# Second half of the value projection moved into the attention's steps, attention output in its own memory, one output bank

## What is computed

```python
q, k, v = jnp.split(h @ w_qkv, 3, axis=-1)          # h: normed tokens; q and k normed by head
# x tokens: neighbourhood plus context
s_nb = einsum('bhqd,bhqkd->bhqk', q_r, k_nb) * NA_SCALE + bias_r
s_ctx = einsum('bhqd,bhkd->bhqk', q_r, kc) * NA_SCALE
p = softmax(concatenate([s_nb, s_ctx], axis=-1))
o = einsum(p[..., :nb], v_nb) + einsum(p[..., nb:], vc)
yx = merge_heads(o) @ w_o
# context tokens (not in layer 3): softmax(qc kc) vc, @ w_o
```

## Time and profile before

| | us |
|---|---|
| median of 3 runs (lowest, highest) | 2507.7 (2506.68, 2511.91) |
| profiled execution, first to last instruction | 2503.2 |
| TensorE busy in it | 2433.3 (97%) |
| DVE / ACT / POOL busy | 1816.1 / 1065.2 / 652.6 |
| heads of layer 0 (203.6 to 302.9) | 99.3 |
| heads of layer 3 (2218.5 to 2279.8) | 61.3 |

### The profile page before, as it was taken

The page is one execution under the profiler, slowest core; times in us unless marked ns, Lnnn a source line. Parts: engine busy times, 40 slices in busy tenths (PEclk is TensorE's granted clock), DMA queues, the critical chain, the costliest instruction groups (busy, mean ns, idle before and its releaser), DMA issues. The chain is left out here.

```text
span 2503.2 us, 36222 instructions
## 1 busy us (share of the span) xinstructions
PE 2433.3 (97%) x12655; PEld 2003.5 (80%) x12655; DVE 1816.1 (73%) x2653; ACT 1065.2 (43%) x1679; POOL 652.6 (26%) x442
## 2 busy tenths in 40 slices
PE   7998899999999999999999999999999999998999
PEld 4675588888888868888888888778888888867999
DVE  4886569888974355427888768987988876855874
ACT  3335534443231244414444227863544324455543
POOL 2414233332300020022333224844333324101000
PEclk9999999999999999999999999999999999999999
DMA  7642025555633321224545542213555554312555
GB/s 270 178 167 76 10 84 171 173 172 192 220 103 101 103 74 51 96 98 135 174 169 173 181 142 77 67 33 111 169 175 168 185 176 125 120 51 68 186 183 186
DMA packets 94890, 337.48 MB, mean 135 GB/s; under 512 B 11840, under 2 KB 13632, under 8 KB 94656
## 3 DMA queue, kind: packets, MB, share of 16 engines
q1 hardware_dynamic: 67136, 240.38, 28.7%
q10 hardware_dynamic: 24768, 86.74, 10.5%
q0 software_dynamic: 2880, 8.92, 1.7%
HBM read 334.95 MB, written 1.05 MB: 134 GB/s over the span
## 5 line engine op out<-in xcount | busy, mean ns | idle before, releaser
L672 PE MATMUL bank<-Hhi,Whi 128*128 128x512 f32 (+1 forms) x2416 | 866.2, 359 | 25.2 <-DVE Wlo L1568 8.4
L674 PE MATMUL bank<-Hhi,Wlo 128*128 128x512 f32 (+1 forms) x2416 | 853.5, 353 | 0.0
L673 PE MATMUL bank<-Hlo,Whi 128*128 128x512 f32 (+1 forms) x2416 | 853.1, 353 | 0.0
L1568 DVE TENSOR_TENSOR Wlo<-raw,Whi 128x1024 fp32r<-128x1024 f32 x424 | 636.4, 1502 | 225.0 <-ACT Whi L1186 207.2
L1186 ACT ACTIVATE Whi<-raw 128x1024 fp32r<-128x1024 f32 x424 | 448.1, 1059 | 749.2 <-DMA raw<-in_weights 695.4
L672 PEld LDWEIGHTS bank<-Hhi,Whi 128*128 128x128 f32 x2416 | 457.1, 189 | 104.1 <-issue 30.5
L673 PEld LDWEIGHTS bank<-Hlo,Whi 128*128 128x128 f32 x2416 | 457.4, 189 | 63.8 <-issue 2.6
L674 PEld LDWEIGHTS bank<-Hhi,Wlo 128*128 128x128 f32 x2416 | 457.4, 189 | 63.0
L545 POOL TENSOR_TENSOR cond_w<-cond_w,cond 128x1024 f32<-128x1024 f32 x107 | 259.3, 2423 | 599.8 <-DVE square L1592 514.7
L672 PE MATMUL bank<-Ghi,Whi 128*128 128x512 f32 (+1 forms) x770 | 268.5, 349 | 0.0
L674 PE MATMUL bank<-Ghi,Wlo 128*128 128x512 f32 (+1 forms) x770 | 266.7, 346 | 0.0
(11 more groups left out here) (267 smaller groups left out, 2990.8 us busy)
## 6 DMA issues: line engine op xcount, KB each, us to landing
raw<-in_weights SPq DMA_DIRECT2D x424, 512.0 KB, 3.4
cond_w<-in_ada ACTq DMA_DIRECT2D x160, 512.0 KB, 3.8
ada_raw<-in_ada SPq DMA_DIRECT2D x16, 512.0 KB, 16.0
ada_ring<-in_ada SPq DMA_DIRECT2D x16, 512.0 KB, 7.4
rel_in<-in_rpb POOLq DMA_DIRECT2D x48, 128.0 KB, 4.8
decay_t<-in_dist POOLq DMA_DIRECT2D x4, 640.0 KB, 4.3
X<-in_x ACTq DMA_DIRECT2D x1, 2048.0 KB, 10.7
out_y<-X SPq DMA_DIRECT2D x1, 1024.0 KB, 4.8
```

What stands on the lines that cost most here:

```text
L672: t.matmul(dst, Whi[:, st.slot, w], hi, start=start, stop=False)
L673: t.matmul(dst, Whi[:, st.slot, w], lo, start=False, stop=False)
L674: return t.matmul(dst, Wlo[:, st.slot, w], hi, start=False, stop=stop)
L1568: v.tensor_tensor(Wlo[:, st.slot, :], raw[:, st.slot, :], Whi[:, st.slot, :].bitcast(F32), ALU.subtract)\
```

## The change

It does four things.

1. Only the first half of V (channels 0 to 511, groups `v+0` to `v+3`) is made ahead of the heads (`values_early`). The second half is made inside the heads' steps, one token block after the other, in bank 7: `late_values(n)`, item n of 32, is one chunk of one block, three matmuls. Layer 0 takes 3, 3, 2 and then 2 items a step, steps 0 to 14; layer 3 takes 3, 3, 2 four times, steps 0 to 11. One item stands between scores and turns, the others behind the turns. ACT alone takes each finished block out (`evict_late`), at the start of its step 3, 7, 11 and 15 (layer 0) or 3, 6, 9 and 12; the next block's first item waits for it.
2. The weight groups `v+4` to `v+7` are all needed until the last block, so their slots come free only then. The splits of `o+0` to `o+2` move to ACT's steps 17, 19, 21 (layer 0; before: two, in steps 5 and 9) and 13, 14, 15 (layer 3; before: none in the heads). DVE follows one step later.
3. The idle transposes are gone. Attend results go to a new tensor `Out` in the place of Q and K, always through bank 6, so an attend waits for the result of the attend **directly** before it.
4. Four of the eight hosted slices move from the value projection and the heads to the output projection's tiles 0, 1, 3 and 4 (`IN_V`, `IN_O`), unshared.

```diff
-IN_V = 8
-V_LATE = 2
-LATE_SPLITS = (5, 9)
+IN_V = 4
+OUT_SPLITS = ((17, 19, 21), (13, 14, 15))
-IN_O = ()
+IN_O = (0, 1, 3, 4)
...
+        self.fill = (3, 3, 2) * TB if self.last else (3, 3, 2) + (2,) * 12
...
+            def values_early(first, tile0):
...
-                tokens_major(p["v"], 2, p["mix_tile"] + 16)
+                values_early(p["v"], p["mix_tile"] + 16)
...
+                def late_values(n):
+                    b, k = divmod(n, C)
+                    st = Step(p["v"] + 4 + k // 2)
+                    if b == 0:
+                        pe.wait_ge(lo_split, st.n + 1)
+                    elif k == 0:
+                        pe.wait_ge(v_made, v0 + 2 + b)
+                    tk = slice(P * b, P * b + P)
+                    last = three_moving(bank[7][:, :], st, slice(512 * (k % 2), 512 * (k % 2) + 512),
+                                        Hhi[:, k, tk], Hlo[:, k, tk], k == 0, k == C - 1)
+                    if b == TB - 1 and k % 2:
+                        last.then_inc(weights_used, 1)
+                    elif k == C - 1:
+                        last.then_inc(v_block, 1)
...
-                    if h.group(n) >= 2:
-                        pe.wait_ge(h_ready, p["o_ready"] + h.group(n) - 1)
+                    if h.group(n) >= 1:
+                        pe.wait_ge(h_ready, p["o_ready"] + h.group(n))
+                    if i >= C // 2:
+                        pe.wait_ge(v_made, v0 + 2 + TB)
...
                     if s == 0:
                         pe.wait_ge(tile_free, FREE0 + p["mix_tile"] + 2 * C + TB)
-                    if s == 1:
-                        pe.wait_ge(tile_free, FREE0 + p["mix_tile"] + 2 * C + 2 * TB)
                     for n in (2 * s, 2 * s + 1):
                         if n < h.n:
                             scores(n)
-                    if s < 4:
-                        idle_products(16 if s == 3 else 5)
+                    items = h.items(s)
+                    for n in items[:1]:
+                        late_values(n)
                     for n in (2 * s - 6, 2 * s - 5):
                         if 0 <= n < h.n:
                             turn(n)
+                    for n in items[1:]:
+                        late_values(n)
...
+                def evict_early():
+                    act.wait_ge(weights_used, p["v"] + 4)
...
+                def evict_late(b):
+                    if b == TB - 1:
+                        act.wait_ge(weights_used, p["v"] + 8)
+                    else:
+                        act.wait_ge(v_block, (TB - 1) * j + b + 1)
+                    a.activation(V[:, b, 512:1024], bank[7][:, :], ACT.Copy).then_inc(v_made, 1)
...
+                evict_early()
+                split(Step(p["v"] + 4))
                 if layer == 0:
-                    evict_v(1)
+                    sum_products(3)
+                    reload(3, p["cond_end"])
...
                 for s in range(h.n // 2 + 5):
+                    if h.block_after(s) is not None:
+                        evict_late(h.block_after(s))
...
+                    if s in h.splits:
+                        split(Step(p["v"] + 5 + h.splits.index(s)))
...
+            def values_early(first, hosts, made):
+                for quarter in range(4):
+                    split(Step(first + quarter))
+                    if hosts:
+                        weigh(quarter, hb[:, :, :].rearrange("p k t -> p (k t)"), follows=quarter >= COND_SLOTS)
+                dve.wait_ge(weights_used, first + 4)
+                for b in range(2):
+                    v.tensor_copy(V[:, b, 0:512], bank[V_BANKS[0][b]][:, :]).then_inc(tile_free, 1)
+                dve.wait_ge(v_made, made + 2)
+                dve.sem_inc(tile_free, 2)
+                split(Step(first + 4))
...
-                    v.tensor_tensor(Hlo[:, i, hs], bank[h.out_bank(i, stream)][:, 0:CTX], Hhi[:, i, hs].bitcast(F32),
+                    v.tensor_tensor(Olo[:, i, hs], bank[6][:, 0:CTX], Ohi[:, i, hs].bitcast(F32),
                                     ALU.subtract).then_inc(h_ready, 1)
```

83 lines of the change are left out of this document (36 added, 47 removed).

## The result

| | before | after |
|---|---|---|
| median of 6 runs, us | 2507.59 (2505.44 to 2511.91) | 2514.72 (2512.36 to 2515.74) |
| profiled execution | 2503.2 | 2510.3 |
| TensorE busy | 2433.3 | 2429.3 |
| DVE / ACT / POOL busy | 1816.1 / 1065.2 / 652.6 | 1820.8 / 1062.0 / 648.6 |

The changed kernel takes 1.003 of the time before, 95% interval 1.0021 to 1.004: slower by 7.1 us, where the prediction said +1.3 and gave the larger chance to "no difference". The time lies in the stated range, 2499 to 2518, but above the forecast's own part of it (2503 to 2512.7): it fell where rival 2, with 2516.5, was expected. Nine more runs of the changed kernel in a later comparison gave 1.0026 (1.0016 to 1.0036).

What follows compares the result with a forecast made beforehand. TensorE, busy 97%, was taken as the bound. Layer 0's +2.3 and layer 3's -0.7 gave +1.6 on the median 2507.7: 2509 us, chance 0.51, own range 2503 to 2512.7, whole range 2499 to 2518.

Steps and rivals of the forecast that it cites:

- rival 2: Single bank becomes the loop of unfilled steps, attends each waiting 0.75 us: +7.5, 2516.5 us; chance 0.23 shared with rival 3.
- Gross gain and start: Filling slack gains 21.5 us gross; heads start 16.8 us earlier in layer 0, 20.2 in layer 3.
- Clock: Layer 0's gap of 5.1 us brings half the clock for 3.4 us, losing 1.7 us; bounds 0 and 3.4.
- Filled steps: Steps 0 to 14 of layer 0 take 54.8 us, steps 0 to 11 of layer 3 53.4, small waits included.
- joints between kinds of matmul: In filled steps, changing from one kind of matmul to another costs 0.7 us in each layer, for some 15 changes.
- Splits: Weight splits in unfilled steps cost 4.2 us in layer 0, 2.5 in layer 3; sum 6.7, bounds 1 and 10.1.
- One output bank: Attends wait for the result directly before, 0.4 us each for five in layer 0, plus both ends: 3.7 us, bounds 1 and 9.
- Hosted slices in the output projection: Four slices make DVE run over by about 1.2 us per tile, unnoticed by TensorE: taken as 0, bound 1.3.
- The rule weighed there: DVE and GpSimd share a port pair under exclusive lock; all eight slice passes would wait for POOL once, sum 1.3 us higher.
- Rival 1: Loop absorbs the splits (6.7 becomes 1) and block boundaries cost nothing (2.8 becomes 0.5): 2501 us; chance 0.26.
- Rival 3: Starts aren't hidden and the fill fails, nothing gained in filled steps: +15 us and more; chance 0.23 shared with rival 2.
- the signs named for a right prediction: TensorE idle 5 and 1.8 us, clock near 0.5, filled steps near 55 and 53, split pairs 12.5 or more, attends waiting for `out_low`.

Runs made afterwards that it cites:

- Evictions ahead of the hosted slice: Changed kernel, in layer 0 evictions of V's first half put ahead of slice 2's sum (ACT) and slice 3's weighing (DVE): 2512.82 us, ratio 1.003.
- holding the clock: Changed kernel plus 36 unread transposes between layer 0's first half of the value projection and the first scores: 2512.37 us, ratio 1.0022.
- the run with fewer joints: The kernel called together, with each step's late items in one run ahead of its turns: 2503.07 us, ratio 0.9984 of the kernel before.
- together: Changed kernel with two output banks after the late items, splits in steps 31, 33, 35 and 15, 17, 19, evictions ahead of split `v+6`: 2497.55 us, ratio 0.9966.

## Why the prediction was right or wrong

**Gross gain and start.** Right. The heads start 16.8 and 20.2 us earlier, with gaps of 5.0 and 1.6 us for 5.1 and 1.8 predicted. The reason given for layer 0's gap was only part of it, as `Evictions ahead of the hosted slice` shows: a split whose load is late stands there too.

**Clock.** The mechanism is right, the size isn't: 1.7 us taken from the earlier trace rows, 2.7 us measured by holding the clock. The lower level lasted 6.8 us, not 3.4, and 6.0 of them lay behind the gap. The bound, 3.4, held. Five other profiles of the same code paid 1.5 to 2.9. And the earlier trace rows shows what came in some profiles only: the wait of 2.25 us of the earlier trace rows is there in all thirteen profiles, and the lower level follows it in five.

**Filled steps.** Layer 0 took 57.7 for 54.8 us. Without the clock's part, 55.0 for 53.1: of 4.4 us beyond the needed 50.6, the three waits for evictions are 2.5 (predicted 1.8) and 1.9 are spread over the steps, 0.1 in a step like that from 239.83 to 243.37 (3.54 us for 3.41 of work; I took 0.7 in all). I named that last part joints between kinds of matmul, and the run with fewer joints doesn't bear it out; its cause stays open. Layer 3: 54.2 for 53.4.

**Splits.** 4.2 and 2.5 us predicted, 3.3 and 1.1 measured. The mechanism is right, and the middle of the heads is the wrong place. By place, the pair with steps 18 to 21, in which the splits of steps 17 and 19 fall, costs 1.1 where I took 2.5, and the next, with step 21's, 2.1 where I took 1.7. Part of it was only covered by the single bank: with two banks layer 0's splits cost 4.5. Layer 3's run into the heads' end, where most of them is hidden.

**One output bank.** 3.7 us predicted, 4.1 measured in the changed kernel (2.9 and 1.2) and 5.4 in the kernel before. Wide attends wait too, which I had at 0, and the last attend of each layer waits 0.9 to 1.0 us longer than before for 0.7. Splits and bank together were taken at 10.4, and are 7.4 + 2.3 = 9.7 with what they cover for each other (the rest of both layers in together against the changed kernel). That this sum came out is partly luck: the edits taken singly give 4.4 for the splits, 2.3 less than I took, and 4.1 for the bank, 0.4 more, and the 1.2 us that each covers for the other were in no term.

**Hosted slices in the output projection.** Taken as 0, measured 1.2, the bound was 1.3. The splits there are indeed far enough ahead, but I looked at TensorE's tiles and not at the norm behind them, which waits for POOL's last sum. The rule weighed there gave +1.3, near what was measured, though four of the eight passes waited for POOL, the second of each slice, and not all eight.

**Rivals.** Rival 1 fell: the splits aren't absorbed. Rival 2 gave 2516.5, close to what was measured, and yet isn't the cause. Its wide and narrow attends all wait, as it said, for 8.2 us in 14 waits, but the price is 4.1, or 5.3 with the splits at the end (layer 0's rest 60.8 to 56.7, layer 3's 25.9 to 24.7), and not 11.2, since part of those waits stands in the place of others. The point from which it decides, 0.3 us more per attend than counted, wasn't reached (4.1 against 3.7 counted is 0.03 for each of 13, 5.3 is 0.12). Rival 3 fell too: the filled steps took 2.9 and 0.8 us more than predicted, not 15. A slip in rival 1: the waits at block boundaries that it lets go were counted with 3.5 us in all (0.4, 1.4, 1.0 and 0.7), not 2.8. The slower result is a sum of small under-estimates on one side: 1.0 (clock), 1.9 (filled steps of layer 0), 0.8 (of layer 3), 1.2 (output projection), and 0.6 outside the stretches; the gaps and the rests of the two layers come out even.

Of the signs named for a right prediction all came but one, filled steps near 55 us in layer 0. Two mechanisms were missed or misplaced, the wait of the norm for POOL and the waits of the wide attends, and the 1.9 us spread over layer 0's filled steps have no known cause. Clock, small waits and slices were taken in the lower part of their bounds, and nothing in the trace said that their errors would cancel.

## What to carry to other kernels

When work is woven into the slack of a loop, price what it pushes out: here the fill itself worked, and the order of the small pieces around it (evictions behind a late load and hosted work, splits in the middle of the heads, one bank for all results) cost more than it gained; with those three put right the same change gains 0.3 to 0.4%. Look for whoever waits behind a stage, not only in it: DVE's lateness in the output projection showed up in the norm. And a wait seen in a trace is not its price, until a run without it shows what comes up behind it.

## What was not expected of the hardware

- The same idle gap of 5.0 to 5.3 us brought 3.4 us at the lower clock in one profile and 6.8 us in five, in these five starting 0.5 to 2.9 us before the gap's end; the price ran from 1.5 to 2.9 us. 36 transposes that nobody reads, 4.09 us of TensorE in that gap, kept the clock up.
- A gap of 1.5 to 1.7 us at the start of the heads had no lower clock behind it in fourteen cases (eleven in layer 3, three in layer 0), a wait of 1.83 us at a block boundary had in one of three, and the wait of 2.25 us in layer 1 in five of thirteen.
- A DVE addition of 2 columns took 0.99 us and a pass of 8 columns 1.14 us while POOL worked, and POOL's total took 2.35 us instead of 1.29 beside a DVE pass: each waited for the other's whole instruction.
